# Decoder layer on one core: moving the first weight difference of the seven-product feed-forward blocks from GpSimd to VectorE

## The chip, the cores and the metric

The kernel runs on one core of a Trainium2 chip (trn2). The metric is device time in microseconds (us) of the whole kernel, the median of several runs. A core has TensorE (PE, matrix products; PEld is its weight load), VectorE (DVE), ScalarE (ACT), GpSimd (POOL) and SyncE (SP, which here only issues transfers). Each engine runs its own instructions in the order in which they are written, and they wait for one another on semaphores.

## The reference, cut to what matters

The layer is a hybrid attention mixer, a cross attention and a feed-forward part, each followed by a layer norm. The change touches the first matrix of the feed-forward part alone (512 tokens, D_MODEL 1024, D_FF 2816, all float32):

```
def swiglu(x, w_in, w_out):
    a, b = jnp.split(x @ w_in, 2, axis=-1)
    return (jax.nn.silu(a) * b) @ w_out
...
    h = swiglu(x, w_ffn_in[l], w_ffn_out[l])
    x = layer_norm(ALPHA * x + h, ln3_g[l], ln3_b[l])
```

## The kernel before

Every float32 product is made of three TensorE passes: both operands are split into a rounded part (`..._hi`) and what is left of it (`..._lo`), and hi·hi, lo·hi and hi·lo are summed in PSUM. ScalarE makes the hi part of a weight tile (a copy that rounds), VectorE the lo part (a subtraction).

`x @ w_ffn_in` has 44 column tiles of 128. The first 8 (N_WHOLE pairs) are computed plainly. The other 36 go in 18 blocks (N_BLOCK) of two tiles: block n covers 256 columns of the weights, even n for `a`, odd n for `b`. In a block both operands are cut into quarters and the product of the 2x2 quarters is made from seven products instead of eight (Strassen-Winograd): P1 to P7, each 4 inner tiles of 3 matmuls of 256 columns, so 84 matmuls a block. The sums of x-quarters are made once; the sums of weight quarters are made in each block:

- T1 = w(0,1) - w(0,0), tile `w_t1` (the trace calls `w_t1` and `w_t2` both `w_t`). It is the right operand of P5. In the kernel before GpSimd makes it (L1009).
- T2 = w(1,1) - T1, tile `w_t2`, VectorE, L1999, operand of P6; T3 = w(1,1) - w(0,1), written over a quarter of `raw`, VectorE, L2000, operand of P7; T4 = w(1,0) - T2, VectorE, L2005, operand of P4. P1, P2 and P3 take quarters of `raw` as they are.

The orders are written out by hand:

- TensorE in block n: P1(n), P4(n-1), P5(n), P3(n-1), P6(n), P2(n), P7(n). Each product (`product`, L2665; matmuls L2691 to L2693) waits for the lo part of its weights (`op_lo`).
- ScalarE (`ffn_block`, L1368): drains a PSUM bank (L1335), hi of P3(n-1), drains another after P1(n) (L1323, "seed"), hi of P6(n), then P2, P7, drains after P6(n) (L1330), hi of P1(n+1), P4(n), P5(n+1); in odd blocks the two silu halves (L1341, L1346) come before the hi of P2(n) and the third (L1356) before that of P4(n). The hi parts are `op_round`, L1314. The hi of P5 waits for `t1_done`.
- VectorE (`ffn_block`, L2044): add_c22 (L2010), lo of P3(n-1), T2, T3, lo of P6(n), P2(n), P7(n), T4, add_c12 (L2016), lo of P1(n+1), then in even blocks from 2 on h_lo (L2041) and the product by silu (`times_second`, L2035), then lo of P4(n), lo of P5(n+1), and in odd blocks L2022. The lo parts are `op_rest`, L1991. Behind block 0 stand also `first_hidden(1, 1)` (L1967, L1969, L1971: the last of the plain tiles) and `sum_rest(4)` (L1983: lo of the x sum for P3).
- Two operand slots per product pair rotate modulo four, so the hi of product m waits for product m-4.
- Transfers: `raw[n % 2]` holds the 1 MB weights of block n. SP issues them in two halves (L883, L884) when the lo of P3(n-2) is done; `half_in` says that the first half, which holds w(0,0) and w(0,1), is there.

Of the kernel before, what the change touches and what calls it, by code (L numbers as in the profile page):

```python
# [43 lines left out]
TT = SEQ // P  # L44
# [94 lines left out]
N_BLOCK = 2 * (D_FF // P // 2 - N_WHOLE)  # L139
# [6 lines left out]
def products_in_order():  # L146

    order = []
    for n in range(N_BLOCK):
        order.append(("P1", n))  # L150
        if n:
            order.append(("P4", n - 1))
        order.append(("P5", n))
        if n:
            order.append(("P3", n - 1))
        order += [("P6", n), ("P2", n), ("P7", n)]
    return order + [("P4", N_BLOCK - 1), ("P3", N_BLOCK - 1)]


PRODUCT = {key: m for m, key in enumerate(products_in_order())}  # L160
LAST = N_BLOCK - 1
# [116 lines left out]
def build_layer(nc, A, out):  # L278
# [11 lines left out]
    n = 0  # L290
# [55 lines left out]
    with ExitStack() as ctx:  # L346
        def sem(name):
            return ctx.enter_context(nc.semaphore(name))

        def sb(name, shape, dt=F32, stack=None):  # L350
            return (stack or ctx).enter_context(nc.sbuf_tensor(name, shape, dt))
# [56 lines left out]
        w_t1 = sb("w_t1", [P, 4, P])  # L408
# [120 lines left out]
        half_in = [sem(f"half_in{i}") for i in range(2)]  # L529
        x_kept, x_whole, sum_done, sum_hi, sum_lo = sem("x_kept"), sem("x_whole"), sem("sum_done"), sem("sum_hi"), sem("sum_lo")  # L530
        t1_done, t2_done, t3_done, t4_done = sem("t1_done"), sem("t2_done"), sem("t3_done"), sem("t4_done")
        op_hi, op_lo, prod_done = sem("op_hi"), sem("op_lo"), sem("prod_done")
# [117 lines left out]
        def w_quarter(n, row, col):  # L650

            k8 = raw[n % 2][:, :].rearrange("p (k c) -> p k c", k=KT)
            return k8[:, 4 * row:4 * row + 4, P * col:P * col + P]

        def right_operand(kind, n):

            if kind == "P1":
                return w_quarter(n, 0, 0)
            if kind == "P2":
                return w_quarter(n, 1, 0)  # L660
            if kind == "P3":
                return w_quarter(n, 1, 1)
            if kind == "P5":
                return w_t1[:, :, :]
            if kind == "P7":
                return w_quarter(n, 0, 1)
            return w_t2[:, :, :]

        def op_slot(m, part):

            w = (w_hi, w_lo)[part][(m + 2) % 4 // 2]
            return quarter(w[:, 512 * (m % 2):512 * (m % 2) + 512])
# [234 lines left out]
        def _(pool):  # L907
# [85 lines left out]
            def widen_cross(pair):  # L993

                c = stat_col("X", 2 * pair, 0)
                pool.wait_ge(rsum_ready, N_OUT - N_AH + pair + 1)
                if pair:
                    pool.wait_ge(recip_ps, N_OUT - N_AH + 1)
                by_head = rsum[:, c:c + 2 * TT].rearrange("p (h t) -> p t h", t=TT)
                pool.tensor_copy(xw[:, :, :].rearrange("p t (h d) -> p t h d", h=2),  # L1000
                                 by_head.unsqueeze(3).to_broadcast([P, TT, 2, DH])).then_inc(recip_wide, 1)

            def weight_sums(n):

                pool.wait_ge(half_in[n % 2], 16 * (1 + n // 2))
                if n:
                    pool.wait_ge(t2_done, n)
                    pool.wait_ge(op_lo, PRODUCT["P5", n - 1] + 1)
                pool.tensor_tensor(w_t1[:, :, :], w_quarter(n, 0, 1), w_quarter(n, 0, 0), ALU.subtract).then_inc(t1_done, 1)  # L1009

            for n in range(3 * TT):
                t = n % TT
                if n == TT:
                    widen_cross(0)
                    widen_cross(1)
                if n == 2 * TT:
                    for b in range(N_BLOCK):
                        weight_sums(b)
                pool.wait_ge(var_done, n + 1)
                pool.tensor_tensor(rstd[:, t:t + 1], var[:, t:t + 1], half[:, 0:1], ALU.pow).then_inc(rstd_done, 1)  # L1020

# [402 lines left out]
        def _(dve):  # L1424
# [8 lines left out]
            def f32(ap):  # L1433
                return ap.bitcast(F32)
# [525 lines left out]
            def first_hidden(i, b):  # L1960

                f = 2 * i + b
                dve.wait_ge(piece_done, 4 * i + PF + b + 3)
                dve.wait_ge(silu_done, f + 1)
                if f:
                    dve.wait_ge(h_done, f)
                dve.tensor_tensor(ht[:, :], ps[:, 2 + b, :], sa[:, b, :], ALU.mult).then_inc(ffn_step, 1)  # L1967
                dve.wait_ge(ffn_step, 2 * f + 1)
                dve.tensor_copy(h_hi[:, f, :], ht[:, :]).then_inc(ffn_step, 1)  # L1969
                dve.wait_ge(ffn_step, 2 * f + 2)  # L1970
                dve.tensor_tensor(h_lo[:, f, :], ht[:, :], f32(h_hi[:, f, :]), ALU.subtract).then_inc(h_done, 1)  # L1971
# [13 lines left out]
            def op_rest(kind, n):  # L1985

                if n > LAST:
                    return
                m = PRODUCT[kind, n]
                dve.wait_ge(op_hi, m + 1)  # L1990
                dve.tensor_tensor(op_slot(m, 1), right_operand(kind, n), f32(op_slot(m, 0)), ALU.subtract).then_inc(op_lo, 1)  # L1991

            def weight_t2(n):

                dve.wait_ge(t1_done, n + 1)
                dve.wait_ge(raw_in[n % 2], F_IN[n % 2] + 16 * (N_WHOLE + 1 + n // 2))
                if n:
                    dve.wait_ge(op_lo, PRODUCT["P4", n - 1] + 1)
                dve.tensor_tensor(w_t2[:, :, :], w_quarter(n, 1, 1), w_t1[:, :, :], ALU.subtract).then_inc(t2_done, 1)  # L1999
                dve.tensor_tensor(w_quarter(n, 0, 1), w_quarter(n, 1, 1), w_quarter(n, 0, 1), ALU.subtract).then_inc(t3_done, 1)  # L2000

            def weight_t4(n):

                dve.wait_ge(op_lo, PRODUCT["P6", n] + 1)
                dve.tensor_tensor(w_t2[:, :, :], w_quarter(n, 1, 0), w_t2[:, :, :], ALU.subtract).then_inc(t4_done, 1)  # L2005

            def add_c22(n):

                dve.wait_ge(u3_done, n + 1)
                dve.tensor_tensor(held(n)[:, HI], bank_b(n), held(n)[:, HI], ALU.add).then_inc(c22_done, 1)  # L2010

            def add_c12(n):

                dve.wait_ge(prod_done, PRODUCT["P3", n] + 1)
                dve.wait_ge(u2_done, n + 1)
                dve.tensor_tensor(held(n)[:, LO], bank_b(n), held(n)[:, LO], ALU.add).then_inc(c12_done, 1)  # L2016
# [7 lines left out]
            def times_right(j):  # L2024

                dve.wait_ge(prod_done, PRODUCT["P4", 2 * j + 1] + 1)
                dve.wait_ge(silu0_done, 2 * j + 2)
                dve.tensor_tensor(sa[:, 0, HI], bank_c(1), sa[:, 0, HI], ALU.mult).then_inc(m0_done, 1)

            def times_second(j):  # L2030

                dve.wait_ge(c22_done, 2 * j + 2)
                dve.wait_ge(c12_done, 2 * j + 2)
                dve.wait_ge(silu1_done, j + 1)
                dve.tensor_tensor(ht[:, :], ht[:, :], sa[:, 1, :], ALU.mult).then_inc(m1_done, 1)  # L2035

            def hidden_rest(j, second):

                f = H_WHOLE + 2 * j + second
                dve.wait_ge(hh_done, 2 * j + second + 1)  # L2040
                dve.tensor_tensor(h_lo[:, f, :], ht[:, :] if second else sa[:, 0, :], f32(h_hi[:, f, :]),  # L2041
                                  ALU.subtract).then_inc(h_done, 1)

            def ffn_block(n):  # L2044

                odd, j = n % 2, n // 2 - 1
                if n:
                    add_c22(n - 1)
                    op_rest("P3", n - 1)
                weight_t2(n)  # L2050
                op_rest("P6", n)
                if not odd and n:
                    times_right(j)
                op_rest("P2", n)
                op_rest("P7", n)
                if odd and n > 1:
                    hidden_rest(j, 1)
                weight_t4(n)
                if n:
                    add_c12(n - 1)  # L2060
                op_rest("P1", n + 1)
                if not odd and n:
                    hidden_rest(j, 0)
                    times_second(j)
                op_rest("P4", n)
                op_rest("P5", n + 1)
                if odd:
                    times_left(n // 2)
# [19 lines left out]
            sum_rest(3)  # L2088
            ffn_rest(1, 3)
            first_hidden(1, 0)  # L2090
            op_rest("P1", 0)
            op_rest("P5", 0)
            for n in range(N_BLOCK):
# [678 lines left out]
```

## Time and profile before

| | us |
|---|---|
| median of 3 runs | 879.09 (878.91 to 879.4) |
| profiled execution, its own time | 879.82 |
| its span in the trace | 878.0 |
| PE, PEld busy | 866.2 (99%), 752.0 (86%) |
| DVE, ACT, POOL busy | 514.7 (59%), 359.6 (41%), 83.9 (10%) |
| chain that ended last | PE 95%, DVE 2% |
| granted TensorE clock | 0.999 of full speed |

The profile is of one execution. Its page gives busy time by engine, the chain of work that ended last and the costliest groups of instructions; the trace behind it gives every instruction with its start, its length and what ended the idle time before it. Successive matmuls overlap in the records: a 256-column matmul is shown as 0.28 us long, and the next starts 0.12 us behind it. The pace is the distance of the starts. The seven-product blocks fill the stretch from 568 to 751 us.

### The profile page before, as it was taken

Reading aid. Unit: us, or ns where it says so; the run is one execution under the profiler, and the core shown is the slowest. Engines: PE = TensorE matmul, PEld = TensorE weight load, DVE = VectorE, ACT = ScalarE, POOL = GpSimd, SP = SyncE. Lnnn points to the kernel's source line nnn. Section 1 sums busy time; section 2 is a strip of 40 time slices with the busy share of each in tenths; the row PEclk is TensorE's granted clock in tenths of the full one; section 3 lists DMA queues with packets and bytes.
Section 4 is the critical chain, followed back from the end, with each engine's and each line's share of the span. In section 5 each row is a group of like instructions: output and inputs, shape, how many; then the busy total and the mean of one; then the engine's idle time right before and its main releaser. Section 6 shows DMA issues by size and latency. Waiting matters only on the chain.

```text
span 878.0 us, 13249 instructions
## 1 busy us (share of the span) xinstructions
PE 866.2 (99%) x5167; PEld 752.0 (86%) x5167; DVE 514.7 (59%) x962; ACT 359.6 (41%) x721; POOL 83.9 (10%) x103
## 2 busy tenths in 40 slices
PE   8999999999999999999999999999999999999996
PEld 8988898877678888888889879899999999888885
DVE  4344347768632626252767589498888888422354
ACT  4112156239642232323335544356665656311221
POOL 3100000081210000000000010111111121000000
PEclk9999999999999999999999999999999999999999
DMA  8535530430003333336423211223233332522211
GB/s 287 164 96 132 132 97 25 144 97 2 1 12 98 100 97 99 97 105 236 163 96 116 77 49 49 97 97 96 98 96 98 123 117 97 184 100 99 102 68 72
DMA packets 70808, 90.36 MB, mean 103 GB/s; under 512 B 3149, under 2 KB 62359, under 8 KB 70751
## 3 DMA queue, kind: packets, MB, share of 16 engines
q1 hardware_dynamic: 70367, 89.15, 31.2%
q8 instruction: 38, 0.62, 0.3%
q0 software_dynamic: 384, 0.43, 0.3%
q14 instruction: 19, 0.16, 0.1%
HBM read 87.05 MB, written 2.52 MB: 102 GB/s over the span
## 4 chain that ended last, share of the span: by engine, by line
PE 95%; DVE 2%; issue 1%; DMA 1%; ACT 1%; SPq 0%; DVEq 0%; POOLq 0%; POOL 0%; ACTq 0%
PE ps L2122 21%; PE ps L2123 21%; PE ps L2124 21%; PE ps L2691 7%; PE ps L2693 7%; PE ps L2692 7%; PE ps L2287 3%; PE ps L2364 3%; PE ps L2324 2%; PE ps L2159 1%; DMA x_nat<-in_x 1%; PE ps L2749 1%; PE ps L2750 1%; PE ps L2751 1%; PE ps L2636 0%
## 5 line engine op out<-in xcount | busy, mean ns | idle before, releaser
L2122 PE MATMUL ps<-xt_hi,w_hi 128*128 128x512 f32 (+1 forms) x400 | 155.6, 389 | 0.3 <-DVE w_lo L1957 0.3
L2124 PE MATMUL ps<-xt_lo,w_hi 128*128 128x512 f32 (+1 forms) x400 | 154.8, 387 | 0.0
L2123 PE MATMUL ps<-xt_hi,w_lo 128*128 128x512 f32 (+1 forms) x400 | 154.8, 387 | 0.0
L1036 ACT CAST w_hi<-raw 128x1024 fp32r<-128x1024 f32 (+1 forms) x57 | 58.9, 1037 | 170.6 <-PE ps L2124 162.1
L1440 DVE TENSOR_TENSOR w_lo<-raw,w_hi 128x1024 fp32r<-128x1024 f32 (+1 forms) x57 | 68.6, 1205 | 90.6 <-ACT w_hi L1036 90.3
L1749 DVE TENSOR_TENSOR w_lo<-raw,w_hi 128x1024 fp32r<-128x1024 f32 x30 | 36.7, 1224 | 90.1 <-ACT w_hi L1203 90.1
L2122 PEld LDWEIGHTS ps<-xt_hi,w_hi 128*128 128x128 f32 x400 | 75.1, 188 | 16.2 <-issue 1.1
L2124 PEld LDWEIGHTS ps<-xt_lo,w_hi 128*128 128x128 f32 x400 | 75.1, 188 | 15.4
L2123 PEld LDWEIGHTS ps<-xt_hi,w_lo 128*128 128x128 f32 x400 | 75.1, 188 | 15.0
L2691 PE MATMUL ps<-xt_hi,w_hi 128*128 128x256 f32 x288 | 81.6, 283 | 0.6 <-ACT ht L1335 0.6
L2692 PE MATMUL ps<-xt_hi,w_lo 128*128 128x256 f32 x288 | 81.5, 283 | 0.0
L2693 PE MATMUL ps<-xt_lo,w_hi 128*128 128x256 f32 x288 | 81.5, 283 | 0.0
L2691 PE MATMUL ps<-s_hi,w_hi 128*128 128x256 f32 x216 | 61.3, 284 | 0.4 <-DVE w_lo L1991 0.3
L2692 PE MATMUL ps<-s_hi,w_lo 128*128 128x256 f32 x216 | 61.1, 283 | 0.0
L2693 PE MATMUL ps<-s_lo,w_hi 128*128 128x256 f32 x216 | 61.1, 283 | 0.0
L1991 DVE TENSOR_TENSOR w_lo<-raw,w_hi 128x512 fp32r<-128x512 f32 x72 | 49.8, 704 | 15.5 <-ACT w_hi L1314 15.3
L2691 PEld LDWEIGHTS ps<-xt_hi,w_hi 128*128 128x128 f32 x288 | 55.3, 192 | 0.8 <-issue 0.7
L2692 PEld LDWEIGHTS ps<-xt_hi,w_lo 128*128 128x128 f32 x288 | 55.3, 192 | 0.0
L2693 PEld LDWEIGHTS ps<-xt_lo,w_hi 128*128 128x128 f32 x288 | 55.3, 192 | 0.0
L2122 PE MATMUL ps<-w_hi,h_hi 128*128 128x512 f32 x136 | 52.9, 389 | 0.0
L2123 PE MATMUL ps<-w_hi,h_lo 128*128 128x512 f32 x136 | 52.9, 389 | 0.0
L2124 PE MATMUL ps<-w_lo,h_hi 128*128 128x512 f32 x136 | 52.9, 389 | 0.0
(346 smaller groups left out, 1852.5 us busy)
## 6 DMA issues: line engine op xcount, KB each, us to landing
raw<-in_w_in SPq DMA_DIRECT2D x24, 1024.0 KB, 5.0
raw<-in_w_ffn_in SPq DMA_DIRECT2D x36, 512.0 KB, 4.4
raw<-in_w_ffn_out SPq DMA_DIRECT2D x11, 1024.0 KB, 4.8
raw<-in_w_mix_out SPq DMA_DIRECT2D x4, 1024.0 KB, 4.8
raw<-in_w_ffn_in SPq DMA_DIRECT2D x4, 1024.0 KB, 5.2
raw<-in_w_branch_b SPq DMA_DIRECT2D x4, 512.0 KB, 4.0
resid<-in_x SPq DMA_DIRECT2D x1, 2048.0 KB, 9.4
raw<-in_w_xkv SPq DMA_DIRECT2D x2, 1024.0 KB, 5.3
```

What stands on the lines that cost most here:

```text
L1036: act.copy(hi, src).then_inc(hi_done, 1)
L1440: dve.tensor_tensor(lo, src, f32(hi), ALU.subtract).then_inc(lo_done, 1)
L1749: dve.tensor_tensor(w_lo[s][:, :].rearrange("p (k c) -> p k c", k=KT), v, f32(w_hi[s][:, :]).rearrange("p (k c) -> p k c", k=KT), ALU.subt ...
L1991: dve.tensor_tensor(op_slot(m, 1), right_operand(kind, n), f32(op_slot(m, 0)), ALU.subtract).then_inc(op_lo, 1)
L2122: pe.matmul(dst, a_hi, b_hi, start=start, stop=False)
L2123: pe.matmul(dst, a_lo, b_hi, start=False, stop=False)
L2124: return pe.matmul(dst, a_hi, b_lo, start=False, stop=stop)
L2287: ins = pe.matmul(ps[:, score_bank(j, b), c0:c0 + cols], q, k, start=True, stop=kind != "C")
L2364: ins = pe.matmul(dst, lhs, rhs, start=start, stop=stop, skip_group_check=True)
L2691: pe.matmul(dst, w_h[:, k, :], x_h[:, k, :], start=clear and k == 0, stop=False, skip_group_check=True)
L2692: pe.matmul(dst, w_l[:, k, :], x_h[:, k, :], start=False, stop=False, skip_group_check=True)
L2693: ins = pe.matmul(dst, w_h[:, k, :], x_l[:, k, :], start=False, stop=k == 3, skip_group_check=True)
```

## The change

GpSimd's function `weight_sums` and its loop over 18 blocks are removed. VectorE gets a function `weight_t1` with the same subtraction on the same tiles and the same waits. For block 0 it stands behind `first_hidden(1, 0)` and ahead of the lo of P1(0); for block n+1 it stands in `ffn_block(n)`, between the lo of P1(n+1) and what follows. After block 17 there is none. TensorE, ScalarE and SP have the same instructions in the same order.

```
-            def weight_sums(n):
-
-                pool.wait_ge(half_in[n % 2], 16 * (1 + n // 2))
-                if n:
-                    pool.wait_ge(t2_done, n)
-                    pool.wait_ge(op_lo, PRODUCT["P5", n - 1] + 1)
-                pool.tensor_tensor(w_t1[:, :, :], w_quarter(n, 0, 1), w_quarter(n, 0, 0), ALU.subtract).then_inc(t1_done, 1)
-
...
-                if n == 2 * TT:
-                    for b in range(N_BLOCK):
-                        weight_sums(b)
...
+            def weight_t1(n):
+
+                if n > LAST:
+                    return
+                dve.wait_ge(half_in[n % 2], 16 * (1 + n // 2))
+                if n:
+                    dve.wait_ge(t2_done, n)
+                    dve.wait_ge(op_lo, PRODUCT["P5", n - 1] + 1)
+                dve.tensor_tensor(w_t1[:, :, :], w_quarter(n, 0, 1), w_quarter(n, 0, 0), ALU.subtract).then_inc(t1_done, 1)
+
...
                 op_rest("P1", n + 1)
+                weight_t1(n + 1)
                 if not odd and n:
                     hidden_rest(j, 0)
                     times_second(j)
...
             first_hidden(1, 0)
+            weight_t1(0)
             op_rest("P1", 0)
```

VectorE's instructions at the end of block 0 and the start of block 1, before: lo of P1(1), of P4(0) and P5(1), the three of `first_hidden(1, 1)`, `sum_rest(4)`, add_c22, lo of P3(0), T2 and T3 of block 1, lo of P6(1).

```order
L1991 TENSOR_TENSOR w_lo<-raw,w_hi 128x512 [waits op_hi]
L1991 TENSOR_TENSOR w_lo<-w_t,w_hi 128x512 [waits op_hi] x2
L1967 TENSOR_TENSOR ht<-ps,sa 128x512 [waits h_done,silu_done,piece_done]
L1969 CAST h_hi<-ht 128x512 [waits ffn_step]
L1971 TENSOR_TENSOR h_lo<-ht,h_hi 128x512 [waits ffn_step]
L1983 TENSOR_TENSOR xt_lo<-sums,xt_hi 128x4x256 [waits sum_hi]
L2010 TENSOR_TENSOR u_a<-ps,u_a 128x256 [waits u3_done]
L1991 TENSOR_TENSOR w_lo<-raw,w_hi 128x512 [waits op_hi]
L1999 TENSOR_TENSOR w_t<-raw,w_t 128x512 [waits op_lo,raw_in1,t1_done]
L2000 TENSOR_TENSOR raw<-raw 128x4x128
L1991 TENSOR_TENSOR w_lo<-w_t,w_hi 128x512 [waits op_hi]
```

The same place now, with line numbers 1 to 11 lower:

```order
L1980 TENSOR_TENSOR w_lo<-raw,w_hi 128x512 [waits op_hi]
L1990 TENSOR_TENSOR w_t<-raw 128x512 [waits op_lo,t2_done,half_in1]
L1980 TENSOR_TENSOR w_lo<-w_t,w_hi 128x512 [waits op_hi] x2
L1956 TENSOR_TENSOR ht<-ps,sa 128x512 [waits h_done,silu_done,piece_done]
L1958 CAST h_hi<-ht 128x512 [waits ffn_step]
L1960 TENSOR_TENSOR h_lo<-ht,h_hi 128x512 [waits ffn_step]
L1972 TENSOR_TENSOR xt_lo<-sums,xt_hi 128x4x256 [waits sum_hi]
L2009 TENSOR_TENSOR u_a<-ps,u_a 128x256 [waits u3_done]
L1980 TENSOR_TENSOR w_lo<-raw,w_hi 128x512 [waits op_hi]
L1998 TENSOR_TENSOR w_t<-raw,w_t 128x512 [waits op_lo,raw_in1,t1_done]
L1999 TENSOR_TENSOR raw<-raw 128x4x128
L1980 TENSOR_TENSOR w_lo<-w_t,w_hi 128x512 [waits op_hi]
```

L1990 is T1 of block 1; everything behind it moved back by one instruction.

The second place is the end of block 2, as of every even block from 2 to 16. VectorE before: T4, add_c12, lo of P1(3), h_lo, the product by silu, lo of P4(2) and P5(3), add_c22.

```order
L2005 TENSOR_TENSOR w_t<-raw,w_t 128x512 [waits op_lo]
L2016 TENSOR_TENSOR ht<-ps,ht 128x256 [waits u2_done,prod_done]
L1991 TENSOR_TENSOR w_lo<-raw,w_hi 128x512 [waits op_hi]
L2041 TENSOR_TENSOR h_lo<-sa,h_hi 128x512 [waits hh_done]
L2035 TENSOR_TENSOR ht<-ht,sa 128x512 [waits silu1_done,c12_done,c22_done]
L1991 TENSOR_TENSOR w_lo<-w_t,w_hi 128x512 [waits op_hi] x2
L2010 TENSOR_TENSOR u_a<-ps,u_a 128x256 [waits u3_done]
```

Now:

```order
L2004 TENSOR_TENSOR w_t<-raw,w_t 128x512 [waits op_lo]
L2015 TENSOR_TENSOR ht<-ps,ht 128x256 [waits u2_done,prod_done]
L1980 TENSOR_TENSOR w_lo<-raw,w_hi 128x512 [waits op_hi]
L1990 TENSOR_TENSOR w_t<-raw 128x512 [waits op_lo,t2_done,half_in1]
L2040 TENSOR_TENSOR h_lo<-sa,h_hi 128x512 [waits hh_done]
L2034 TENSOR_TENSOR ht<-ht,sa 128x512 [waits silu1_done,c12_done,c22_done]
L1980 TENSOR_TENSOR w_lo<-w_t,w_hi 128x512 [waits op_hi] x2
L2009 TENSOR_TENSOR u_a<-ps,u_a 128x256 [waits u3_done]
```

Three instructions now stand between the lo of P1(3) and that of P4(2), where two stood.

## Rows read from the trace of the kernel before

**Rows 1.** Stretch: length; PE, PEld, DVE, ACT, POOL busy (count); clock, DMA, GB/s.

```profile
588.00:740.00 152.00, 152.00 (x1269) 152.00 (x1268) 133.21 (x220) 90.67 (x187) 25.05 (x15) 1.00 0.33 105
```

**Rows 2.** What TensorE's weight loads waited for, 540 to 770: us, times, longest.

```profile
PEld ps L2691 <- DVE w_lo L1991: 0.8, 2, 0.5
PEld ps L2691 <- issue: 0.7, 1, 0.7
```

**Rows 3.** TensorE by time (start, length): first of P3(0), first two of P6(1).

```profile
579.92 0.28 PE L2691 MATMUL ps<-xt_hi,w_hi 128*128 128x256 f32 x1
...
581.65 0.39 PE L2691 MATMUL ps<-s_hi,w_hi 128*128 128x256 f32 x1
581.87 0.28 PE L2692 MATMUL ps<-s_hi,w_lo 128*128 128x256 f32 x1
```

**Rows 4.** VectorE in order of time, blocks 0 and 1.

```profile
573.84 0.69 DVE L1991 TENSOR_TENSOR w_lo<-raw,w_hi 128x512 fp32r<-128x512 f32 x1 [0.90 <-ACT w_hi L1314]
574.45 1.31 DVE L1991 TENSOR_TENSOR w_lo<-w_t,w_hi 128x512 fp32r<-128x512 f32 x2
575.67 0.68 DVE L1967 TENSOR_TENSOR ht<-ps,sa 128x512 f32<-128x512 f32 x1
576.39 0.43 DVE L1969 CAST h_hi<-ht 128x512 fp32r<-128x512 f32 x1
...
578.93 0.68 DVE L1991 TENSOR_TENSOR w_lo<-raw,w_hi 128x512 fp32r<-128x512 f32 x1
579.53 0.68 DVE L1999 TENSOR_TENSOR w_t<-raw,w_t 128x512 f32<-128x512 f32 x1
...
580.90 0.69 DVE L1991 TENSOR_TENSOR w_lo<-w_t,w_hi 128x512 fp32r<-128x512 f32 x1
```

**Rows 5.** ScalarE in order of time, blocks 0 and 1.

```profile
569.52 0.36 ACT L1323 COPY ps<-ps 128x256 f32<-128x256 f32 x1 [5.68 <-PE ps L2693]
...
573.71 1.33 ACT L1314 CAST w_hi<-w_t 128x512 fp32r<-128x512 f32 x2
...
580.25 0.62 ACT L1314 CAST w_hi<-w_t 128x512 fp32r<-128x512 f32 x1 [2.25 <-DVE w_t L1999]
```

**Rows 6.** VectorE in order of time, end of an even block (block 6).

```profile
634.70 0.69 DVE L1991 TENSOR_TENSOR w_lo<-raw,w_hi 128x512 fp32r<-128x512 f32 x1 [0.37 <-ACT w_hi L1314]
635.31 0.68 DVE L2041 TENSOR_TENSOR h_lo<-sa,h_hi 128x512 fp32r<-128x512 f32 x1
...
636.52 1.29 DVE L1991 TENSOR_TENSOR w_lo<-w_t,w_hi 128x512 fp32r<-128x512 f32 x2
```

**Rows 7.** TensorE: first matmul of P4(6), then the start of P4(8).

```profile
637.90 0.28 PE L2691 MATMUL ps<-xt_hi,w_hi 128*128 128x256 f32 x1
...
657.94 0.28 PE L2693 MATMUL ps<-xt_lo,w_hi 128*128 128x256 f32 x1
658.05 0.33 PE L2691 MATMUL ps<-xt_hi,w_hi 128*128 128x256 f32 x1
658.22 0.28 PE L2692 MATMUL ps<-xt_hi,w_lo 128*128 128x256 f32 x1
```

**Rows 8.** VectorE, lo of P4(8) and P5(9).

```profile
657.27 1.28 DVE L1991 TENSOR_TENSOR w_lo<-w_t,w_hi 128x512 fp32r<-128x512 f32 x2
```

**Rows 9.** VectorE, end of an odd block (block 7): lo of P4(7), P5(8).

```profile
646.27 1.29 DVE L1991 TENSOR_TENSOR w_lo<-w_t,w_hi 128x512 fp32r<-128x512 f32 x2 [0.66 <-ACT w_hi L1314]
```

**Rows 10.** VectorE groups by form, 560 to 752 us: busy us, mean ns, idle before.

```profile
L1991 DVE TENSOR_TENSOR w_lo<-raw,w_hi 128x512 fp32r<-128x512 f32 x72 | 49.8, 704 | 15.5 <-ACT w_hi L1314 15.3
...
L2005 DVE TENSOR_TENSOR w_t<-raw,w_t 128x512 f32<-128x512 f32 x18 | 21.1, 1174 | 0.0
...
L1999 DVE TENSOR_TENSOR w_t<-raw,w_t 128x512 f32<-128x512 f32 x18 | 12.3, 684 | 0.0
```

**Rows 11.** GpSimd's T1 and VectorE's T4 in block 2.

```profile
591.65 1.48 POOL L1009 TENSOR_TENSOR w_t<-raw 128x512 f32<-128x512 f32 x1 [6.64 <-DMA raw<-in_w_ffn_in]
...
591.90 1.78 DVE L2005 TENSOR_TENSOR w_t<-raw,w_t 128x512 f32<-128x512 f32 x1
```

## The prediction

> **What bounds the kernel now.** I read first the busy table by stretch [rows 1]: from 588 to 740 us TensorE and its weight load are busy for all of 152.00 us, VectorE for 133.21, ScalarE for 90.67. TensorE sets the pace, with no gap. VectorE is close behind it: at 84 matmuls of 0.12 us a block takes 10.1 us, the stretch holds 15, and VectorE works 8.8 us of each. Then the list of what TensorE waited for [rows 2]: in the whole seven-product stage its weight loads waited twice for VectorE (P6(0) and P6(1), 0.8 us together) and once near the end, 0.7 us. So an instruction more on VectorE costs nothing until it makes a lo part late for TensorE, and one less on GpSimd gives nothing back unless it ends a wait. The reader is to see where slack is small, and that is a matter of order, not of sums.
>
> How TensorE starts again behind a wait is in the rows of P6(1) [rows 3]. P3(0) starts at 579.92, twelve matmuls of 0.12 us later P6(1) was due, at 581.36. Its lo part ends at 580.90 + 0.69 = 581.59 [rows 4] and the matmul starts at 581.65, 0.06 later. The second starts 0.22 behind it where the pace is 0.12: a weight load that could not run ahead costs 0.10 more. Loss there now: 0.29 + 0.10 = 0.39 us.
>
> **The change, part by part.** VectorE's new subtraction has the form of the ones beside it, 0.68 us long with the next start 0.60 to 0.61 behind (579.53 after 578.93 [rows 4], 635.31 after 634.70 [rows 6]). So one T1 takes a slot of 0.60 and its result is there 0.68 after its start. GpSimd took 1.48 for one [rows 11], beside everything else.
>
> *T1 of block 0.* It delays the lo of P1(0) and P5(0) and the T2 behind them by some 0.6 to 1.2 us. ScalarE then has nothing to do before 569.52, where it had been idle for 5.68 us, waiting for TensorE's P1(0) [rows 5]; the next hi part, of P6(0), stands behind that drain. It hides all of it. Cost 0. Were that idle time gone, it would cost up to 1.2.
>
> *T1 of block 1.* Here there is no cover: from 573.84 VectorE works without a pause up to the lo part that TensorE waits for at 581.65 [rows 4]. Step by step: T1 starts 0.60 behind the lo of P1(1), at 574.45, and ends at 575.13. The lo of P4(0) moves from 574.45 to 575.05. ScalarE made the hi of P4(0) and P5(1) in one go from 573.71 [rows 5]; now the hi of P5(1) has to wait for T1: 575.17 to 575.79 (0.04 from a VectorE end to a ScalarE start, as from 580.21 to 580.25 [rows 4, 5]). The lo of P5(1) starts at 575.82 instead of about 575.07, and L1967 at 576.42 instead of 575.67: 0.75 later, 0.60 for T1 and 0.15 for the hand-over. All that follows is VectorE's own queue, so the lo of P3(0) goes from 578.93 to 579.68 and ends at 580.36. P3(0) was due at 579.92 [rows 3] and its lo had been there at 579.61; now TensorE waits there too: release 580.42, loss 0.50 + 0.10 = 0.60. The old wait moves with T2: 580.28 to 580.96, hi of P6(1) 581.00 to 581.62, lo 581.65 to 582.34, P6(1) at 582.40 instead of 581.65. Both waits lie on one chain; together they are what P6(1) is late: **+0.75 us**. Nothing behind absorbs it, since TensorE paces the rest, and the wait near the end [rows 2] is behind a drain of TensorE's own result, so it moves along.
>
> *T1 in the even blocks 2 to 16 (eight of them).* The lo of P1(n+1) starts when ScalarE's hi is ready, which hangs on TensorE's P6(n) and doesn't move: 634.70 in block 6 [rows 6]. Behind it stand now T1, h_lo, the product by silu, and the lo of P4(n), which so goes from 636.52 to 637.12 and ends at 637.81. P4(6) is due at 637.90 [rows 7]. That is 0.09 ahead, and whether it is enough is to be read in the same trace: in block 8 the lo of P4(8) ended at 657.27 + 0.69 = 657.96 [rows 8], 0.10 ahead of the due start 658.06; the matmul came at 658.05 but took 0.33, and the next started at 658.22 in place of 658.18 [rows 7]. So 0.10 ahead costs 0.04, since the weight load wants to run a matmul early. With 0.09 ahead I take 0.05. The pattern repeats in all eight with the same distance of 3.20 us between the two starts, but for block 8, where the distance is 3.16, 0.04 is paid already and 0.09 would be. Sum 8 x 0.05 = **+0.40 us**. Since each hangs anew on TensorE's P6(n), the losses add up. Bounds: 0 (the load ahead just fits) and 0.15 each (the result comes 0.10 later than reckoned).
>
> *T1 in the odd blocks.* The lo of P4(n) had waited 0.66 us for ScalarE [rows 9]; T1 fits in that gap, and the hi of P5(n+1) has over 1 us in hand. Early in odd blocks what stands behind the even block's T1 is 0.6 late (T2, hi and lo of P6); that had 1.5 us to TensorE's start, 0.9 remains, and the waits for ScalarE end the lateness. The transfers that SP issues behind the lo of P3 start 0.6 later in these blocks and had over a microsecond. Cost 0.
>
> *GpSimd's part removed.* No later GpSimd instruction waited for it. What goes is a disturbance: T4 takes 0.68 as T2 does, and 1.78 when it meets GpSimd's T1 [rows 10, 11]. By the groups [rows 10] T4 took 21.1 us where T2, of the same form, took 12.3: 8.8 us lost, and the lo parts from `raw` lost 72 x (0.704 - 0.684) = 1.4. So **10.2 us come back on VectorE** against 18 x 0.605 = 10.9 added. They lie ahead of the lo of P1(n+1), which waits for ScalarE in any case (0.37 idle ahead of it [rows 6]), so TensorE gets nothing. In block 2 T4 began at 591.90, GpSimd was done at 593.13, and T4 ended 0.55 later [rows 11]. The section "SBUF: two separate sides" of the Trainium skill's page "SBUF — State Buffer" says that a GpSimd instruction that reads SBUF and a VectorE one with two SBUF inputs exclude each other for a whole instruction; the trace agrees, and by that rule alone the change is a swap of nearly equal parts (rival C).
>
> **Sum.** 0.75 + 0.40 = 1.15 us on the profiled execution's 879.82: 880.97. That execution was 0.73 above the median 879.09, and carried over to the median the forecast is 880.24, so **880.2 us**, 0.13% more. With the bounds of the even blocks (0 and 1.2) the likeliest case has 879.8 to 881.0.
>
> **The rivals.** About 0.2% (1.76 us, 880.85) is what a measurement can tell from no change.
>
> *A, slower: the margin in the even blocks is overdrawn.* I let the next instruction start 0.60 behind T1. Where one needs the result of the one before, VectorE starts it only behind the other's end, 0.72 after its start (L1967 at 575.67, L1969 at 576.39 [rows 4]). If T1, with its three waits, holds what follows it in the same way, the lo of P4 is 0.12 later and every even block pays 0.17: 8 x 0.17 = 1.36, and block 1 pays 0.87. Sum 2.2: 881.3. It decides from a slot of 0.68 on, where 8 x 0.13 + 0.83 passes 1.76. Against it: T2 has three waits as well and starts 0.60 behind its forerunner [rows 4].
>
> *B, nothing arrives.* The even blocks fit, and something in block 1 gives way: 0.0 to 0.5 us, 879.3. Against it: at P6(1) VectorE is the one waited for.
>
> *C, VectorE's total decides* (the swap above): lateness that no wait clears would carry on from block to block, 10.9 - 10.2 = 0.7 us in the end, 879.8. Rows 1 speak against it, with 1.2 us idle on VectorE in each block, but a transfer that lands late could use that up.
>
> *D, faster: the exclusion had cost TensorE time.* All waits of this stage are 1.5 us [rows 2] and three restarts at 0.10, 1.8 with them, and none but the 0.04 at P4(8) stands behind GpSimd. Even all of it would give 877.3.
>
> **How the numbers follow.** Forecast 0.64, A 0.17, B 0.10, C 0.07, D 0.02. The range takes in the forecast's own 879.8 to 881.0, B's 879.3 and A's 881.3, and 0.2 us on each side by which the runs of before differ: 879.1 to 881.5. Slower by over 0.2%: A, and 0.03 from the upper end of the forecast: 0.20. Faster: D, 0.02. The rest, 0.78, is within 0.2%.
>
> **What would show it.** P3(0) starts with a wait of about half a microsecond, and P6(1) at some 582.4. The first matmul of P4 in blocks 2 to 16 is longer than 0.28, and the second 0.17 behind it or more, while TensorE still shows 152 of 152 us busy, as such a loss is too short for a gap. ScalarE waits for VectorE's T1 in block 1. T4 takes 0.69 in all 18 blocks, VectorE's busy time hardly moves, and GpSimd's 25.05 us of rows 1 are gone. Wrong would be: P4 as before in the even blocks (then B), waits of 0.2 and more there (A), or a new wait for a transfer.

## The result and the profile after

| | before | after |
|---|---|---|
| median (12 runs each), us | 879.35 | 881.00 |
| profiled execution, its own time | 879.82 | 880.84 |
| its span | 878.0 | 879.1 |
| ratio after/before | | 1.0017, 95% interval 1.0009 to 1.0024 |

The change makes the kernel slower by 0.17%, about 1.5 us by the ratio and 1.65 by the medians. The forecast was +1.15.

To see where the time went I use one length in every trace: the **stage**, from the first matmul of P1(0) to the first matmul of the second matrix. Ahead of it the kernels here differ in nothing but T1 of block 0, and the stage's start still differs by up to 1.3 us from execution to execution (567.0 to 568.3; after the change it came 0.64 earlier than before), so spans don't compare well and stages do. Before, the stage runs from 567.88 to 751.03, 183.15 us; after, from 567.24 to 752.08, 184.84: **1.69 longer**. Inside it, each step between matmul starts that is not 0.12 us is a loss, and they can be listed one by one:

| place | lost before | lost after | difference |
|---|---|---|---|
| P6(0) | 0.53 | 0.53 | 0 |
| P4(0), P3(0), P6(1): the chain of block 1 | 0.39 | 1.16 | +0.77 |
| P4(n), eight even blocks | 0.05 (block 8 alone) | 8 x 0.06 = 0.50 | +0.45 |
| P4(17), the drain behind P7(17) | 0.78 | 0.87 | +0.09 |
| P3(17), the stage's last product | 0 | 0.44 | +0.44 |
| sum | 1.75 | 3.50 | +1.75 |

The sum is 0.06 above the difference of the stages, since other steps are a hundredth under or over 0.12.

The weight loads' waits, which answer to [rows 2] (us in all, times, longest), and the busy table of the steady blocks, which answers to [rows 1] (length; PE, PEld, DVE, ACT, POOL busy with counts; clock, DMA share, GB/s), after the change:

```profile
PEld ps L2692 <- DVE w_lo L1980: 2.5, 5, 0.8
```

```profile
588.00:740.00 152.00, 152.00 (x1266) 151.98 (x1265) 132.53 (x234) 90.46 (x187) 0.00 (x0) 1.00 0.33 105
```

TensorE waits four times for a lo part in place of two: at P6(0), P3(0), P6(1) and P3(17). The fifth and longest in that row, 0.8, is the weight load of P4(17). Its lo part was ready at 748.07 and the load began at 748.68; the matmul's own row names ScalarE's drain, and in the trace of before the same wait of 0.7 stood under "issue". VectorE has 14 instructions more in that stretch and is busy 0.68 us less: it has back what its meetings with GpSimd's T1 had taken. The groups that answer to [rows 10] (busy us, mean ns, idle before) show the same:

```profile
L1980 DVE TENSOR_TENSOR w_lo<-raw,w_hi 128x512 fp32r<-128x512 f32 x72 | 48.6, 687 | 19.3 <-ACT w_hi L1303 18.1
...
L1990 DVE TENSOR_TENSOR w_t<-raw 128x512 f32<-128x512 f32 x18 | 12.3, 685 | 0.0
L2004 DVE TENSOR_TENSOR w_t<-raw,w_t 128x512 f32<-128x512 f32 x18 | 12.3, 685 | 0.0
```

T4 (L2004) is down from 21.1 us to 12.3, the lo parts from `raw` from 49.8 to 48.6: 10.0 us back against 12.3 busy, or 10.9 in slots, added.

Block 1 on VectorE, which answers to [rows 4] (start, length; the stage starts 0.64 earlier here, so 573.80 is 574.44 on the clock of before):

```profile
573.80 0.68 DVE L1990 TENSOR_TENSOR w_t<-raw 128x512 f32<-128x512 f32 x1
574.40 1.47 DVE L1980 TENSOR_TENSOR w_lo<-w_t,w_hi 128x512 fp32r<-128x512 f32 x2
575.78 0.68 DVE L1956 TENSOR_TENSOR ht<-ps,sa 128x512 f32<-128x512 f32 x1
...
581.01 0.69 DVE L1980 TENSOR_TENSOR w_lo<-w_t,w_hi 128x512 fp32r<-128x512 f32 x1
```

and ScalarE there, which answers to [rows 5]: the wait for T1 ahead of the hi of P5(1).

```profile
574.52 0.62 ACT L1303 CAST w_hi<-w_t 128x512 fp32r<-128x512 f32 x1 [0.84 <-DVE w_t L1990]
...
575.99 0.37 ACT L1324 COPY u_a<-ps 128x256 f32<-128x256 f32 x1
```

TensorE at P4(0), P3(0), P6(1) and at P4(2), the places of [rows 3] and [rows 7]:

```profile
576.50 0.35 PE L2692 MATMUL ps<-xt_hi,w_hi 128*128 128x256 f32 x1
...
579.78 0.39 PE L2692 MATMUL ps<-xt_hi,w_hi 128*128 128x256 f32 x1 [0.17 <-DVE w_lo L1980]
...
581.76 0.39 PE L2692 MATMUL ps<-s_hi,w_hi 128*128 128x256 f32 x1 [0.29 <-DVE w_lo L1980]
...
597.70 0.34 PE L2692 MATMUL ps<-xt_hi,w_hi 128*128 128x256 f32 x1
597.88 0.28 PE L2693 MATMUL ps<-xt_hi,w_lo 128*128 128x256 f32 x1
```

The two waits of the forecast are there, and the step from 597.70 to 597.88 instead of 597.82 is the 0.06 of an even block; it repeats at 618, 638, 658, 679, 699, 719 and 739.

In block 2 the lo of P4(2) runs from 596.92 to 597.61 (by the 0.69 of such an instruction), 0.09 ahead of 597.70, as reckoned.

**The stage's end** is what the forecast did not have. VectorE and ScalarE in block 17, before:

```profile
743.13 0.68 DVE L2041 TENSOR_TENSOR h_lo<-ht,h_hi 128x512 fp32r<-128x512 f32 x1
743.74 0.68 DVE L2005 TENSOR_TENSOR w_t<-raw,w_t 128x512 f32<-128x512 f32 x1
744.34 0.42 DVE L2016 TENSOR_TENSOR u_a<-ps,u_a 128x256 f32<-128x256 f32 x1
...
746.29 0.69 DVE L1991 TENSOR_TENSOR w_lo<-w_t,w_hi 128x512 fp32r<-128x512 f32 x1 [1.53 <-ACT w_hi L1314]
...
748.72 0.68 DVE L1991 TENSOR_TENSOR w_lo<-raw,w_hi 128x512 fp32r<-128x512 f32 x1
...
745.12 0.63 ACT L1356 ACTIVATE sa<-u_a 128x512 f32<-128x512 f32 x1
...
747.57 0.37 ACT L1335 COPY ht<-ps 128x256 f32<-128x256 f32 x1 [0.36 <-PE ps L2693]
```

and after:

```profile
744.82 0.69 DVE L2004 TENSOR_TENSOR w_t<-raw,w_t 128x512 f32<-128x512 f32 x1
745.43 0.42 DVE L2015 TENSOR_TENSOR u_a<-ps,u_a 128x256 f32<-128x256 f32 x1
...
747.38 0.69 DVE L1980 TENSOR_TENSOR w_lo<-w_t,w_hi 128x512 fp32r<-128x512 f32 x1 [1.54 <-ACT w_hi L1303]
...
748.33 1.23 DVE L1429 TENSOR_TENSOR s_lo<-raw,s_hi 128x1024 fp32r<-128x1024 f32 x1
...
749.80 0.68 DVE L1980 TENSOR_TENSOR w_lo<-raw,w_hi 128x512 fp32r<-128x512 f32 x1
...
746.21 0.63 ACT L1345 ACTIVATE sa<-u_a 128x512 f32<-128x512 f32 x1 [0.60 <-DVE u_a L2015]
746.74 0.60 ACT L1303 CAST w_hi<-w_t 128x512 fp32r<-128x512 f32 x1
747.25 1.04 ACT L1025 CAST s_hi<-raw 128x1024 fp32r<-128x1024 f32 x1
748.20 0.36 ACT L1324 COPY ht<-ps 128x256 f32<-128x256 f32 x1
...
750.54 0.39 PE L2692 MATMUL ps<-xt_hi,w_hi 128*128 128x256 f32 x1 [0.18 <-DVE w_lo L1980]
```

T1 of block 17, made in block 16, leaves VectorE 0.55 us late against TensorE: add_c12 starts 1.09 later, of which TensorE's own shift is 0.54. ScalarE's silu waits for it (0.60), and from there the delay takes two roads. On ScalarE come the hi of P4(17), the first weight tile of the second matrix (1.04) and only then the drain behind P7(17): before, that drain had waited 0.36 for TensorE, now it starts without a wait, and P4(17) loses 0.09 more. VectorE waits for the hi of P4(17) until 747.38, 1.09 later than before, and then works without a pause: the lo of P4(17), L2021, the lo of the second matrix's tile (1.23), add_c22 and the lo of P3(17), which starts 1.08 later than before (749.80 for 748.72) where TensorE is 0.63 later. It ends at 750.48, and TensorE, due at 750.21, waits. The drain is not what holds this lo part: it had ended at 748.56, add_c22 starts at 749.47.

### The profile page after: what moved, and what is told of

Its sections match the earlier page's. It is cut to its first block, busy times and chain, and to the rows that moved or that the text cites. A ratio compares the mean times of both kernels' runs of the same rounds, so it can differ in the third digit from the quotient of the medians.

```text
span 879.1 us, 13249 instructions
## 1 busy us (share of the span) xinstructions
PE 866.8 (99%) x5167; PEld 752.2 (86%) x5167; DVE 516.4 (59%) x980; ACT 359.0 (41%) x721; POOL 53.0 (6%) x85
## 4 chain that ended last, share of the span: by engine, by line
PE 93%; DVE 3%; issue 2%; ACT 1%; DMA 1%; SPq 0%; DVEq 0%; POOLq 0%; POOL 0%; ACTq 0%
PE ps L2123 21%; PE ps L2125 21%; PE ps L2124 21%; PE ps L2692 6%; PE ps L2694 6%; PE ps L2693 6%; PE ps L2288 3%; PE ps L2365 3%; PE ps L2325 2%; PE ps L2160 1%; DMA x_nat<-in_x 1%; PE ps L2750 1%; PE ps L2751 1%; PE ps L2752 1%; DVE w_lo L1980 1%
## 5 line engine op out<-in xcount | busy, mean ns | idle before, releaser
L1980 DVE TENSOR_TENSOR w_lo<-raw,w_hi 128x512 fp32r<-128x512 f32 x72 | 48.6, 687 | 19.3 <-ACT w_hi L1303 18.1
```

## The experiments

All kernels are read by the stage, and timed against the kernel before on the same chip.

| run | stage, us | stage less before | ratio to before, 95% |
|---|---|---|---|
| the kernel before | 183.15 | | |
| the changed kernel | 184.84 | +1.69 | 1.0017 (1.0009 to 1.0024) |
| e1_t1_of_1_on_gpsimd | 184.09 | +0.94 | 1.0018 (1.0008 to 1.0027) |
| e2_t1_of_17_on_gpsimd | 185.45 | +2.30 | 1.0013 (1.0003 to 1.0023) |
| e9_c12_first | 184.95 | +1.80 | 1.0015 (1.0006 to 1.0025) |
| e5_t1_twice | 191.40 | +8.25 | 1.0098 (1.0081 to 1.0115) |
| e3_t1_behind_p4 | 192.52 | +9.37 | 1.0104 (1.0087 to 1.0121) |
| e8_all_mended | 191.05 | +7.90 | 1.0087 (1.0073 to 1.0102) |
| e6_before_cover_moved | 182.21 | -0.94 | 0.9986 (0.9977 to 0.9995) |
| e7_after_cover_moved | 183.30 | +0.15 | 0.9997 (0.9988 to 1.0006) |
| e10_t1_ahead_of_p1 | 183.13 | -0.02 | 0.9999 (0.9990 to 1.0008) |
| e11_ahead_and_cover | 182.21 | -0.94 | 0.9989 (0.9980 to 0.9998) |

The stage is of one execution, the ratio of many. The traced execution need not be a typical one: that of e1 was the fastest of its ten (879.85, median 880.72), that of e2 the slowest of its ten (881.51, median 880.48).

### Block 1 alone

GpSimd has its function back and calls it for block 1 only.

```
+                if n == 2 * TT:
+                    for b in (1,):
+                        weight_sums(b)
...
-                if n > LAST:
+                if n > LAST or n in (1,):
                     return
```

> The changed kernel, but GpSimd makes T1 of block 1 (as before), VectorE the other 17. Measure: the stage from the first matmul of P1(0) to the first matmul of the second matrix, 183.15 us before and 184.85 us after the change. Theory of the margins (each place pays for itself): the chain to P6(1) is free of T1 and of the hand-over, P6(1) starts 13.77 us behind P1(0) as before (14.53 after), P3(0) no longer waits, and the stage is 184.1. Theory of VectorE's total: one T1 of 18 is worth 0.1 us, the stage is 184.75.

Measured: 184.09. P6(1) starts at 580.77, 13.77 behind P1(0) as before, and P4(0) and P3(0) start without a loss:

```profile
580.36 0.28 PE L2705 MATMUL ps<-xt_lo,w_hi 128*128 128x256 f32 x1
580.77 0.39 PE L2703 MATMUL ps<-s_hi,w_hi 128*128 128x256 f32 x1
580.99 0.28 PE L2704 MATMUL ps<-s_hi,w_lo 128*128 128x256 f32 x1
```

One T1 of 18 carries 0.75 of 1.69 us. That rules out a cost by VectorE's total, where it would be a tenth. The even blocks' 0.06 and the end's losses stand unchanged in this trace. The timed ratio doesn't show the 0.75: its interval is 1.7 us wide, and the ten runs lie in two groups, 879.85 to 880.42 and 881.03 to 881.97, and the trace is of the fastest. What sets the groups apart no trace shows.

### The stage's end

First T1 of block 17 on GpSimd, by the same edit with `(17,)`.

> The changed kernel, but GpSimd makes T1 of block 17, the last one (it is made in block 16). Margins, as corrected by the trace of the changed kernel: in block 16 the first matmul of P4(16) is no longer late (0.06), and in block 17 T2, T4 and add_c12 are on time, so silu, the hi of P4(17), the drain behind P7(17) and the lo of P3(17) are too; the wait of P3(17) for VectorE (0.18 idle, about 0.42 lost) is gone and P4(17) waits 0.09 less: the stage is 184.3 instead of 184.85. If instead the end of the stage were late for its transfer or for the shifted clock of everything before, it stays at 184.8.

Measured: 185.45, longer, not shorter. The end did as the margins said: P4(16) has no loss, P4(17) lost 0.78 as before the change, and P3(17) nothing. But TensorE lost 1.23 us around block 8 in this execution, 0.26 at P1(9) and 0.97 at P4(8), where the changed kernel's trace has 0.06. Without that excess of 1.17 the stage is 184.28, where 184.3 was expected. What happened there is in ScalarE's and TensorE's rows:

```profile
655.74 0.62 ACT L1314 CAST w_hi<-raw 128x512 fp32r<-128x512 f32 x1 [1.07 <-PE ps L2705]
656.27 0.61 ACT L1314 CAST w_hi<-w_t 128x512 fp32r<-128x512 f32 x1
```

```profile
657.15 0.39 PE L2703 MATMUL ps<-xt_hi,w_hi 128*128 128x256 f32 x1
659.55 0.39 PE L2703 MATMUL ps<-xt_hi,w_hi 128*128 128x256 f32 x1 [0.71 <-DVE w_lo L1991]
```

The drain ahead of it had ended at 654.68, so the hi of P1(9) began 1.07 late. The row names TensorE as what it waited for, but the half transfer for T1 and P1 of block 9 was issued at 649.12 and landed 6.6 us later, at 655.7, where most take 3.4 to 3.7; and in the next run, e9, the same instruction was 0.46 late and the row names the transfer.

To test which road the end's loss takes, that run leaves all T1 on VectorE and moves one instruction of block 17.

```
+                if n == LAST:
+                    add_c12(n - 1)
                 if odd and n > 1:
                     hidden_rest(j, 1)
                 weight_t4(n)
-                if n:
+                if n and n < LAST:
                     add_c12(n - 1)
```

> The changed kernel, but in block 17 alone VectorE does add_c12 of block 16 ahead of h_lo and T4. All T1 stay on VectorE and T2 of block 17 is as late as after the change. If the loss at the stage's end runs over add_c12, silu and the hi of P4(17): add_c12 ends 1.2 earlier, the lo of P3(17) is on time and the stage is 184.35. If it runs over T4 or over the transfer for the second matrix: 184.85.

Measured: 184.95, with 0.63 lost in block 8; less that excess of 0.57 it is 184.38. The waits of TensorE from 740 us on:

```profile
PE ps L2694 <- ACT ht L1324: 0.6, 1, 0.6
```

No wait for VectorE is left there, P4(17) lost 0.79, and P3(17) nothing. So the end's loss starts at add_c12 and runs over silu and the hi of P4(17); T4, which stood later here than in the changed kernel, and the transfer for the second matrix are not on it. In block 8 of this run ScalarE waited for the transfer:

```profile
ACT w_hi L1303 <- DMA raw<-in_w_ffn_in: 0.5, 1, 0.5
```

### The even blocks: dose and place

T1 made twice, the first time with a semaphore of its own.

```
+                dve.tensor_tensor(w_t1[:, :, :], w_quarter(n, 0, 1), w_quarter(n, 0, 0), ALU.subtract).then_inc(t1_first, 1)
+                dve.wait_ge(t1_first, n + 1)
                 dve.tensor_tensor(w_t1[:, :, :], w_quarter(n, 0, 1), w_quarter(n, 0, 0), ALU.subtract).then_inc(t1_done, 1)
```

> The changed kernel, with each T1 made twice in a row on VectorE, the second behind the end of the first: a slot of 1.32 us instead of 0.60. Margins: each even block pays the further 0.72 in full, since nothing is left of its margin (8 x 0.72 = 5.8), block 1 pays 0.72, block 0 and the odd blocks nothing as far as their slack goes: stage 184.85 + 6.5 = 191.3, plus up to 0.7 at its end. VectorE's total: 18 x 0.72 = 13.0 more work against 1.2 us idle per block, 21 us in all, so that theory lets most of it vanish: 185 to 187.

Measured: 191.40. Each even block lost 0.79 (0.06 + 0.73), block 1's chain 0.74 more than after the change, odd blocks nothing. VectorE in block 2:

```profile
596.27 0.69 DVE L1981 TENSOR_TENSOR w_lo<-raw,w_hi 128x512 fp32r<-128x512 f32 x1 [0.95 <-ACT w_hi L1304]
596.88 0.69 DVE L1991 TENSOR_TENSOR w_t<-raw 128x512 f32<-128x512 f32 x1
597.60 0.69 DVE L1993 TENSOR_TENSOR w_t<-raw 128x512 f32<-128x512 f32 x1
598.21 0.69 DVE L2043 TENSOR_TENSOR h_lo<-sa,h_hi 128x512 fp32r<-128x512 f32 x1
```

The margin is used up exactly, and VectorE's idle time of 0.95 us just ahead of the chain is of no use to it. Behind a real dependence the slot is 0.72 (596.88 to 597.60), behind T1 as the change has it 0.61.

Next the same work one place later: in even blocks T1 behind the lo of P4(n).

```
                 op_rest("P1", n + 1)
-                weight_t1(n + 1)
+                if odd or not n:
+                    weight_t1(n + 1)
...
                 op_rest("P4", n)
+                if not odd and n:
+                    weight_t1(n + 1)
                 op_rest("P5", n + 1)
```

> The changed kernel, but in the even blocks from 2 on VectorE makes T1 behind the lo of P4(n), not ahead of h_lo; the same work, one place later. Margins: the lo of P4(n) is on time again, so all eight first matmuls of P4 are 0.28 long and the 0.06 of each is back, 0.48 us; the hi and lo of P5(n+1) come some 1.5 us later and had over 1 us, which may just be too little; the end of the stage stays late, since T2 and what follows it in block 17 are as late as after the change. Stage 184.4. Rival: the eight short losses come from something else that went with GpSimd's part (the pace of TensorE's reads), then they stay: 184.85.

Measured: 192.52, 7.7 us longer than the changed kernel where 0.5 shorter was expected. The cause is in the list of TensorE's waits and in ScalarE's rows:

```profile
PE ps L2695 <- ACT u_a L1324: 6.5, 8, 0.8
```

```profile
594.48 0.62 ACT L1303 CAST w_hi<-w_t 128x512 fp32r<-128x512 f32 x1
597.75 0.62 ACT L1303 CAST w_hi<-w_t 128x512 fp32r<-128x512 f32 x1 [2.65 <-DVE w_t L1990]
598.27 0.37 ACT L1324 COPY u_a<-ps 128x256 f32<-128x256 f32 x1
```

ScalarE stands before the hi of P5(3) for 2.65 us, and behind that instruction in its queue is the drain after P7(2), for which P4(2) waits. I had looked at P5's own slack and not at what is queued behind it. All eight even blocks lost 1.05 us each. The same road explains the loss at P4(0) in the changed kernel: ScalarE waited 0.84 for T1, and its drain ended at 576.36, 0.14 ahead of the start of P4(0), which had been due at 576.39; at P4(17) the start is 0.14 to 0.15 behind the drain's end too. The run e8 has this edit, that of e9 and the one of the next section.

> All T1 on VectorE, none on GpSimd, with three reorderings: that of the stage's start; T1 behind the lo of P4(n) in even blocks; in block 17 add_c12 ahead of h_lo and T4. Margins: each place of the change is hidden, stage 184.85 - 1.68 - 0.48 - 0.5 = 182.2, that is 0.95 less than the kernel before and 0.1% faster than it.

Measured: 191.05. It has no loss up to P4(2), and none at P3(17), but 1.05 us in seven of the even blocks and 1.55 in block 8.

### The cover of block 1

At the stage's start, ScalarE makes the hi of P6(0) and of the fourth x sum ahead of its first drain, and VectorE the lo of that sum in the gap behind the lo of P6(0).

```
-                seed(n)
+                if n:
+                    seed(n)
                 op_round("P6", n)
+                if n == 0:
+                    sum_round(4)
+                    seed(n)
...
                 ffn_block(n)
-                if n == 0:
-                    sum_round(4)
...
                 op_rest("P6", n)
+                if n == 0:
+                    sum_rest(4)
...
                     first_hidden(1, 1)
-                    sum_rest(4)
```

On the kernel before:

> The kernel before (GpSimd makes T1), but at the start of the seven-product stage ScalarE makes the hi of P6(0) and of the fourth x sum ahead of its drain behind P1(0), and VectorE makes the lo of that sum behind the lo of P6(0) instead of behind first_hidden(1, 1). This takes 1.2 us out of VectorE's chain to P6(1) and the drain out of P6(0)'s. Margins: the waits of before at P6(0) (0.43 + 0.10) and at P6(1) (0.29 + 0.10) are gone; stage 183.15 - 0.92 = 182.2, time 0.1% less than before. Rival: the waits only move to the next product, stage 183.1.

Measured: 182.21. Both waits for VectorE are gone, and the only one left is:

```profile
PE ps L2694 <- ACT ht L1335: 0.6, 1, 0.6
```

On the changed kernel:

> The changed kernel with the same reordering at the stage's start. Margins: T1 of block 1 now has cover (1.2 us taken out of the chain, 0.75 put in), so its 0.76 is gone as well as the two waits of before: stage 184.85 - 0.76 - 0.92 = 183.15, the same as before the change; the even blocks' 0.06 and the end's 0.5 remain. If T1 of block 1 costs its time whatever stands around it: 183.9.

Measured: 183.30. Nothing is lost before P4(2). T1 of block 1 still takes its slot and makes ScalarE wait, but the lo of P6(1) now ends 12.82 us behind the start of P1(0) (at 580.27, the stage starting at 567.45) instead of 14.46:

```profile
573.50 0.68 DVE L1992 TENSOR_TENSOR w_t<-raw 128x512 f32<-128x512 f32 x1
574.10 1.47 DVE L1982 TENSOR_TENSOR w_lo<-w_t,w_hi 128x512 fp32r<-128x512 f32 x2
...
579.58 0.69 DVE L1982 TENSOR_TENSOR w_lo<-w_t,w_hi 128x512 fp32r<-128x512 f32 x1
```

So T1 of block 1 cost its time only for want of cover. Of the 183.30, 0.12 is again the late transfer: it landed after 5.5 us, and P4(8) lost 0.18 instead of 0.06.

### T1 where VectorE waits anyway

```
-                op_rest("P1", n + 1)
                 weight_t1(n + 1)
+                op_rest("P1", n + 1)
```

> All T1 on VectorE, but one instruction earlier: T1 of block n+1 ahead of the lo of P1(n+1), in the stretch in which VectorE waits for ScalarE anyway (0.90 us in block 0, 1.47 in the even blocks of the changed kernel, 0.32 in odd ones, where T4 is now unstretched and the lateness of the even block gone), not behind it. Margins: T1 is hidden at every place; P6(1), the P4 of the even blocks and the end of the stage are as before the change: stage 183.1 to 183.2, time within 0.1% of the kernel before. If VectorE's total or T1's presence were what costs: 184.8.

Measured: 183.13. One instruction earlier, the same 18 subtractions on VectorE cost nothing. Block 6:

```profile
632.48 0.42 DVE L2015 TENSOR_TENSOR ht<-ps,ht 128x256 f32<-128x256 f32 x1
632.82 0.68 DVE L1990 TENSOR_TENSOR w_t<-raw 128x512 f32<-128x512 f32 x1
634.37 0.69 DVE L1980 TENSOR_TENSOR w_lo<-raw,w_hi 128x512 fp32r<-128x512 f32 x1 [0.87 <-ACT w_hi L1303]
```

VectorE is 0.87 us idle behind T1 and ahead of the lo of P1(7), which has to wait for ScalarE. The list of losses is that of the kernel before, without the 0.05 of block 8. Three times T1 waited for its transfer, 1.2 us in all, and that was hidden too. With the reordering at the stage's start besides:

> The kernel of the run e10 with the reordering at the stage's start of the run e6 besides. Margins: stage 182.2 as there, with GpSimd doing nothing in it; time 0.1% less than before.

Measured: 182.21, median 878.40 against 879.43, ratio 0.9989 (0.9980 to 0.9998). Together with e6 (0.9986) it is the fastest, faster than both kernels, and the two can't be told apart (the same stage): in these orders it makes no difference who makes T1.

## Why the prediction was right

The likeliest case was +1.15 us, with 0.75 to 1.95 by the bounds of the even blocks; it came to +1.69 in the stage and 1.5 to 1.65 in the timed runs, within the range. Step by step:

- **What bounds the kernel** held: TensorE's pace, broken only where a lo part is late. e1, e7 and e10 show that T1 of block 1 costs 0.75 or 0 by its place in the order and by what stands around it.
- **T1 of block 0**, cost 0: held. P6(0) lost 0.53 before and after.
- **T1 of block 1**, +0.75: held, P6(1) started 14.52 us behind P1(0) instead of 13.77. Two details were wrong. ScalarE's drain behind P7(0) was late as well, so P4(0) already lost 0.19 and P3(0) 0.43 instead of 0.60. And T1's hand-over also worked as said: the two lo parts behind it took 1.47 instead of 1.31.
- **T1 in the even blocks**, 8 x 0.05: the loss was 0.06 each, 0.50 in all, 0.45 more than before. The reading of block 8 in the trace of before as a gauge for so small a margin was good to 0.01.
- **T1 in the odd blocks**, cost 0: **this step failed, for block 17.** It said that the waits for ScalarE end the lateness of 0.6 us that the even block leaves behind. They don't: ScalarE's hi parts hang on T2 and are as late. In the odd blocks up to 15 there is enough slack towards TensorE. In block 17 the first tile of the second matrix stands in the queues besides: its hi ahead of ScalarE's last drain (0.09 lost), its lo ahead of the lo of P3(17) on VectorE (0.44 lost). Cost 0.53. e2 and e9 show it from two sides.
- **GpSimd's part removed**: 10.0 us came back on VectorE where 10.2 were reckoned, and TensorE got 0.05 at most. The amount was right, and the balance of VectorE, rival C, was not what counted: e5 paid 0.73 per even block with VectorE idle for 0.95 just ahead.
- **Rival A** fell: the slot of T1 is 0.60, not 0.72. **B** fell by the waits at P3(0) and P6(1) and by e1. **D**: the removal gave nothing.
- The size is 0.54 short, and that is the missed step at the end. The measured 881.00 still lies at the upper end of the likeliest case, 879.8 to 881.0, but that end was reckoned with 0.15 for each even block, which did not come, and 0.26 of it is the median of before, 879.35 here for 879.09. That the number fits so well is in part luck.

A part of the cost in the timed runs is open: how often the transfer for block 9 is late enough to add to it. In the traces of e2 and e9, where it landed after 6.6 and 6.0 us, it cost 1.17 and 0.57 us, in e7 (5.5) 0.12, in that of the changed kernel, where it landed after 4.1, nothing. In the order of the change T1 stands between that transfer and the lo of P4(8), so a late one should cost up to 0.6 more than before. That is argued from the rows and not measured by itself; what the traces show is that about the same lateness cost 0.18 in block 8 of e7, 0.05 in the kernel before (5.4) and nothing in e10 (5.2), where T1 stands one place earlier.

## What to carry to other kernels

An instruction moved to a busy in-order engine costs nothing or its whole length by its place in the queue: look for the gap in which that engine waits for another, and put it there if its inputs arrive in time (e10 against the change: one line moved, 1.7 us). Follow each delay not only to its consumer but to what is queued behind the consumer on that engine. The largest miss here (e3, +7.7 us) was a drain behind a waiting instruction on ScalarE; of the missed 0.53 us at the stage's end, 0.09 was such a drain, and 0.44 was a lo part four places behind the one with which VectorE waited for ScalarE. And walk the last block of a loop by itself, as its neighbours are others.

## What the runs showed of the hardware that I had not expected

- TensorE's restart has two prices here. Behind a late weight tile the step to the second matmul is 0.22 us instead of 0.12 (+0.10, at P6(0), P3(0), P6(1), P3(17)); behind a late PSUM drain, with the lo part long there, it is 0.19 to 0.20 (+0.07 to 0.08, at P4(17) in all traces and at P4 in e3). The weight load had not run ahead in the second case either: at P4(17) it starts 0.03 ahead of its matmul (748.05 and 748.08 before the change), at P3(0) together with it (579.78 after the change). A lo part that ends 0.09 to 0.10 ahead of the due start costs 0.05 to 0.07, with no wait shown. The rows of the weight loads fit it: in the steady stream each load starts together with the matmul before its own, 0.12 ahead, and that of P4(2) started at 597.66 instead of 597.58.
- The half transfer for T1 and P1 of block 9, needed in block 8, lands late in every trace: 4.0 to 4.1 us behind its issue in those of the changed kernel, e1 and e5, 4.7 to 6.6 in the others, where most of the other halves take 3.4 to 3.7. Before the change it was issued at 648.86 and GpSimd, waiting for it, started at 654.29, 5.4 us later, against 3.6 in block 6 (628.25 to 631.86). In five of the twelve traces a half issued near 619 or 679 us takes 4.6 us or more too, up to 5.8 (e11). What delays it is open.

```profile
648.86 0.37 SPq L883 DMA_DIRECT2D raw<-in_w_ffn_in  x1
```

```profile
654.29 1.30 POOL L1009 TENSOR_TENSOR w_t<-raw 128x512 f32<-128x512 f32 x1 [10.16 <-DMA raw<-in_w_ffn_in]
```
